# The mixture-of-experts stage of a float32 network: experts ranked on chip, run in pairs of a large and a small one, the four smallest in two matrix passes instead of three

## The chip, the cores and the metric

The kernel runs on one core of one Trainium2 chip. The metric is the device time of one execution in microseconds (us). Before the change it is 1656.29 us, the median of three runs (1655.75 to 1657.96). Engines are named as in the profile: PE is the matrix engine (PEld its weight loads), DVE the vector engine, ACT the scalar engine, POOL the GpSimd engine, SP the engine that issues most transfers.

## The reference, cut to what matters

Two blocks of a network are computed for 256 tokens of width 1024, in float32. All but the last stage stay as they are. The last stage is a mixture of experts: each token goes to its two best of eight experts, and the outputs are added with softmax gates; then a layer norm follows.

```python
def moe_swiglu(h, router, wg, wu, wd):
    logits = (t @ router)
    vals, idx = lax.top_k(logits, TOP_K)            # TOP_K = 2 of N_EXPERTS = 8
    gates = softmax(vals)
    combine = sum(one_hot(idx, N_EXPERTS) * gates[..., None], 1)
    for e in range(N_EXPERTS):                      # D_EXPERT = 1408
        out += combine[:, e:e + 1] * swiglu(t, wg[e], wu[e], wd[e])

def swiglu(t, wg, wu, wd):
    return (silu(t @ wg) * (t @ wu)) @ wd
h = layer_norm(ALPHA * h + out, ln2_g, ln2_b)
```

The 256 tokens choose 512 times in all. Worked out from the reference for the inputs drawn with seed 0, the eight experts get 110, 80, 89, 28, 21, 35, 109 and 40 tokens.

## The kernel before

**Weights.** All weights of the kernel come as one stream of 311 units of 1 MB, each 16 tiles of 128x128 in float32. A unit's way is: SP loads it into one of four buffers `stg` (NS = 4); ACT copies it, rounded to the PE's one-pass float format, to `wh` (one of three buffers, NW = 3, line 1223); DVE writes the remainder `wl = stg - wh` (line 1723); PE multiplies. ACT may write `wh` of unit u only when PE is done with unit u-3 (the semaphore event `("unit", u - NW)`), and SP may load unit u only when ACT and DVE are both done with unit u-4. The activations are split in the same way into a high and a low part, and each product is made of three matmuls: high x `wh`, low x `wh`, high x `wl` (lines 981 to 983 for gate and up, 1012 to 1014 for down). ACT and DVE run their splits at fixed places of their programs: the class `Splits` issues the split of unit u+2 where the walk over the tiles enters unit u.

**Experts.** They begin with unit 179 (`EXPERT_UNIT`); one takes 16.5 units: for gate and up, 11 column tiles in groups of 4, 4 and 3 (`GU`), each with 8 steps over the width, and for down 11 steps for each of two halves of 512 columns. `route()` finds each token's two experts, its place in the expert's list (`rk`) and the longest list (`CNT`). If this is at most 128, the arm `sparse()` runs, otherwise `every_token()`, in which each expert takes all 256 tokens. In `sparse()` the tokens of an expert are gathered by matmuls with a selection matrix `SE` (line 1053; from `XTH` and `XTL` to `GH` and `GL`, 128 rows an expert, whatever its count), and the results go back through `SX` (`ST` in the rows; `scatter`, lines 1065 and 1066), which DVE adds to `RES` (line 2348). The tokens are the stationary operand of the matmuls (128 columns of it), the weights stream. Between gate/up and down stand silu on ACT (line 1602), the product with up on DVE (`hidden`, line 2323), its transposition on PE (`turn`, line 962), and the split of the result on ACT (line 1586) and DVE (line 2306). `select` (lines 1037, 1039) makes `SX` and the token's gate `CO`. The eight experts run one after another, in their own order; scatter, gather and select of neighbours are put between the groups of gate/up.

**What sets the order.** Each engine's program is written out by hand, and each engine runs its own in order; there is no scheduler. A wait in front of an instruction holds back everything behind it on that engine.

Of the kernel before, what the change touches and what calls it, by code (L numbers as in the profile page):

```python
# [8 lines left out]
F32 = mybir.dt.float32  # L9
F32R = mybir.dt.float32r  # L10
# [5 lines left out]
P = 128  # L16
# [99 lines left out]
class Dry:  # L116
# [14 lines left out]
    def __le__(self, other):  # L131
        return self
# [33 lines left out]
DOWN = [(0, kt) for kt in range(8)] + [(1, kt) for kt in range(8)] + [(0, kt) for kt in range(8, 11)] + [(1, kt) for kt in range(8, 11)]  # L166
# [7 lines left out]
def low_event(j, q):  # L174
    return "gathered_low_a" if j == 0 and q >= 2 else "gathered_low"
# [13 lines left out]
def model_kernel(nc, w_d, x_d, meta_d, small_d, const_d, look_d, tab1_d, tab2_d, out_d):  # L189
# [3 lines left out]
    with ctx:  # L193
# [79 lines left out]
        with ExitStack() as st:  # L273
            C8 = sb("C8", [P, 10, 2, 8], F32, st)
            CNT = sb("CNT", [P, 9], F32, st)
            CNI = sb("CNI", [P, 1], I32, st)
            XTH = sb("XTH", [P, 2, D], F32R, st)
# [4 lines left out]
            with ExitStack() as sp:  # L282
                SX = [sb(f"ST{i}", [P, S], F32R, sp) for i in range(2)]
                GH = [sb(f"GH{i}", [P, KD, 2 * P], F32R, sp) for i in range(2)]
                GL = [sb(f"GL{i}", [P, KD, 2 * P], F32R, sp) for i in range(2)]
                SHH = [sb(f"SHH{i}", [P, 11, P], F32R, sp) for i in range(2)]
                SHL = [sb(f"SHL{i}", [P, 11, P], F32R, sp) for i in range(2)]
                CO = sb("CO", [P, 2], F32, sp)
# [112 lines left out]
        def tensor_program(w, pe):  # L401
# [506 lines left out]
            def route():  # L908
# [41 lines left out]
                keep_warm(3)  # L950

            def gate_up(tag, x, nT, lh, ll, operand, turned, between):
                pend = []

                def turn():
                    while pend:
                        gi, n0, nn, i, j = pend.pop(0)
                        b, old = bank((tag, "ht", x, gi, i), (f"h_low_{tag}", (x, gi, i)))
                        vacant(old)
                        w.wait_ge(*m.of(f"hidden_{tag}", (x, gi, i)))  # L960
                        for c in range(nn):
                            ins = pe.transpose(PS[b][:, c * P:(c + 1) * P], mtm2[j][:, c * P:(c + 1) * P], ident)
                        ins.then_inc(*m.inc(f"group_{tag}", ("ht", x, gi, i)))

                for gi, (n0, nn) in enumerate(GU):
                    for up in range(2):
# [1775 lines left out]
```

## Time and profile before

| what | before |
|---|---|
| median of three runs | 1656.29 us |
| span of the profiled execution, first to last instruction | 1654.0 us |
| experts' stage (first expert matmul to the last) | 1229.2 to 1635.3 us |
| two experts with all that stands between them | 102.6 us |
| PE busy in the stage | all of it but about 1 us |
| granted PE clock | 1.00 to the last stretch |

The profiled execution has no time of its own beside its span; the 2.3 us between span and median are taken as what lies around the span, and the sum is made against the span and carried over to the median. A matmul's duration in a row is longer than its share of PE, since matmuls overlap: what one costs is the distance between two starts. DVE and ACT rows carry some 0.08 us of tail, which the next instruction overlaps.

### The profile page before, as it was taken

The numbers are of one execution on the slowest core, as the hardware profiler recorded it, in microseconds if no ns is written. First come the engines' busy times: TensorE is split into PE (matmuls) and PEld (weight loads), VectorE is DVE, ScalarE is ACT, GpSimd is POOL, SyncE is SP. The second block draws the span as 40 slices with busy tenths as digits, with TensorE's granted clock in tenths as the row PEclk, the third lists the DMA queues.
The fourth block names the chain that finished last, engine by engine and source line by source line (L and its number), as shares of the span: only waits on it lengthen the run. The fifth ranks groups of instructions, "written<-read, shape, count | busy, mean of one in ns | idle before, by whom it ended". The sixth has DMA issues, their size and how long they took to land.

```text
span 1654.0 us, 27617 instructions
## 1 busy us (share of the span) xinstructions
PE 1622.1 (98%) x11068; PEld 1477.6 (89%) x11068; DVE 1241.3 (75%) x1766; ACT 972.3 (59%) x1381; POOL 309.1 (19%) x307
## 2 busy tenths in 40 slices
PE   8999999999999999999999999999999999999997
PEld 6988888898888889998999999999998888888886
DVE  5565776656567656898875554799988898898897
ACT  6556675446657634555554443555558677777675
POOL 1231552123217501143120002132110000000000
PEclk9999999999999999999999999999999999999999
DMA  8632455555235554543435544543428898988993
GB/s 289 234 115 103 168 189 194 181 199 183 110 133 198 179 202 176 177 150 114 168 119 190 176 179 178 170 154 128 179 100 340 328 352 340 340 333 330 351 342 126
DMA packets 50198, 339.76 MB, mean 205 GB/s; under 512 B 5576, under 2 KB 7840, under 8 KB 10352
## 3 DMA queue, kind: packets, MB, share of 16 engines
q1 hardware_dynamic: 47344, 328.79, 54.0%
q0 software_dynamic: 2720, 9.13, 1.8%
q8 instruction: 91, 1.49, 0.4%
q14 instruction: 43, 0.34, 0.1%
HBM read 336.76 MB, written 1.13 MB: 204 GB/s over the span
## 4 chain that ended last, share of the span: by engine, by line
PE 90%; DVE 4%; ACT 3%; POOL 1%; issue 1%; DMA 0%; SPq 0%; DVEq 0%; POOLq 0%; ACTq 0%
PE bank L549 12%; PE bank L523 8%; PE bank L525 8%; PE bank L524 8%; PE bank L547 7%; PE bank L981 5%; PE bank L982 5%; PE bank L983 5%; PE bank L680 3%; PE bank L682 3%; PE bank L681 3%; PE bank L1014 2%; PE bank L1013 2%; PE bank L1012 2%; DVE wl L1723 1%
## 5 line engine op out<-in xcount | busy, mean ns | idle before, releaser
L1723 DVE TENSOR_TENSOR wl<-stg,wh 128x2048 fp32r<-128x2048 f32 x310 | 712.7, 2302 | 212.0 <-ACT wh L1223 209.8
L1223 ACT ACTIVATE wh<-stg 128x2048 fp32r<-128x2048 f32 x310 | 592.6, 1912 | 180.2 <-PE bank L983 82.5
L523 PE MATMUL bank<-xx,wh 128*128 128x272 f32 (+1 forms) x778 | 225.6, 290 | 0.0
L525 PE MATMUL bank<-xx,wl 128*128 128x272 f32 (+1 forms) x778 | 223.3, 287 | 0.0
L524 PE MATMUL bank<-xx,wh 128*128 128x272 f32 (+1 forms) x778 | 223.1, 287 | 0.0
L549 PE MATMUL bank<-xx,wh 128*128 128x512 f32 x448 | 159.7, 396 | 0.0
L549 PE MATMUL bank<-H,wh 128*128 128x512 f32 x434 | 151.3, 390 | 0.0
L524 PEld LDWEIGHTS bank<-xx,wh 128*128 128x128 f32 x778 | 147.5, 190 | 0.0
L981 PE MATMUL bank<-wh,GH 128*128 128x512 f32 (+3 forms) x400 | 147.5, 369 | 0.0
L523 PEld LDWEIGHTS bank<-xx,wh 128*128 128x128 f32 x778 | 146.3, 188 | 1.1 <-issue 0.7
L982 PE MATMUL bank<-wh,GL 128*128 128x512 f32 (+3 forms) x400 | 146.5, 366 | 0.0
L525 PEld LDWEIGHTS bank<-xx,wl 128*128 128x128 f32 x778 | 146.3, 188 | 0.0
L983 PE MATMUL bank<-wl,GH 128*128 128x512 f32 (+3 forms) x400 | 146.1, 365 | 0.0
L680 PE MATMUL bank<-wh,xx 128*128 128x256 f32 x480 | 139.7, 291 | 1.4 <-DVE zm L1797 0.8
L682 PE MATMUL bank<-wl,xx 128*128 128x256 f32 x480 | 134.7, 281 | 0.0
L681 PE MATMUL bank<-wh,xx 128*128 128x256 f32 x480 | 134.5, 280 | 0.0
L547 PE MATMUL bank<-xx,wl 128*128 128x256 f32 x512 | 132.4, 279 | 0.1
L547 PE MATMUL bank<-H,wl 128*128 128x256 f32 x448 | 124.0, 282 | 0.0
L2525 POOL TENSOR_TENSOR fu<-ft 128x256 f32<-128x256 f32 x64 | 84.9, 1330 | 134.2 <-ACT ft L1371 134.2
L2083 DVE SCALAR_TENSOR_TENSOR CA<-HC,small,CA 128x272 f32<-128x272 f32 x240 | 107.4, 500 | 0.7
L547 PEld LDWEIGHTS bank<-xx,wl 128*128 128x128 f32 x512 | 96.5, 188 | 5.9 <-issue 0.3
L680 PEld LDWEIGHTS bank<-wh,xx 128*128 128x128 f32 x480 | 90.2, 188 | 12.0 <-issue 9.0
(386 smaller groups left out, 3550.7 us busy)
## 6 DMA issues: line engine op xcount, KB each, us to landing
stg<-in_w SPq DMA_DIRECT2D x310, 1024.0 KB, 4.8
BT<-bias_scratch POOLq DMA_DIRECT2D x3, 1024.0 KB, 11.4
BT<-bias_scratch POOLq DMA_DIRECT2D x1, 2048.0 KB, 12.8
BB<-bias_scratch POOLq DMA_DIRECT2D x2, 1024.0 KB, 6.3
res<-in_x SPq DMA_DIRECT2D x1, 1024.0 KB, 6.4
stg<-in_w SPq DMA_DIRECT2D x2, 512.0 KB, 7.9
BB<-bias_scratch POOLq DMA_DIRECT2D x2, 512.0 KB, 7.0
out<-res SPq DMA_DIRECT2D x4, 256.0 KB, 3.1
```

What stands on the lines that cost most here:

```text
L523: pe.matmul(out, wh, xh(kt), start=kt == 0, stop=False)
L524: pe.matmul(out, wh, xl(kt), start=False, stop=False)
L525: ins = pe.matmul(out, wl, xh(kt), start=False, stop=kt == KT - 1)
L547: ins = pe.matmul(PS[b][:, 0:S], wl, high(kt), start=False, stop=False)
L549: ins = pe.matmul(out, wh, both(kt), start=False, stop=kt == KT - 1)
L680: pe.matmul(out, xh_t(kt, tt), wh, start=kt == 0, stop=False)
L682: ins = pe.matmul(out, xh_t(kt, tt), wl, start=False, stop=kt == KD - 1)
L981: pe.matmul(out, lh(kt, i), wh, start=kt == 0, stop=False)
L982: pe.matmul(out, ll(kt, i), wh, start=False, stop=False)
L983: ins = pe.matmul(out, lh(kt, i), wl, start=False, stop=kt == KD - 1)
L1223: act.activation(WH[u % NW][:, :], stg[u % NS][:, :], ACT.Copy).then_inc(*m.inc("w_high", u))
L1723: vec.tensor_tensor(WL[u % NW][:, :], stg[u % NS][:, :], WH[u % NW][:, :].bitcast(F32), ALU.subtract).then_inc(*m.inc("w_low_v", u))
```

## The change

1. **Ranking.** After the router, DVE orders the experts by their counts: expert 0 is put first always (its first weights are loaded before the counts are known), the others follow by count (`TIE`, `CNT`, `POS`, `PERM`). The arm `sparse()` is taken if each of the first four has at most 128 tokens and each of the last four at most 64 (`TWICE`, `NEED`).
2. **Pairs.** The experts run as four pairs (rank 0 with 4, 1 with 5, 2 with 6, 3 with 7). Within a pair the groups alternate: gate and up of a column group for the large one, then for the small one; in down they change after every 4 steps, which is one unit.
3. **Two passes.** A small expert's 64 tokens stand twice in the stationary operand, 64 columns of high and 64 of low parts, so that high x `wh`, low x `wh`, high x `wl` and low x `wl` take two matmuls (`in_two`). The two halves of the result are added by a plain float32 matmul with a stacked identity (`BOTH`, `turn_and_sum`), which also transposes; for it ACT copies both results from the bank to `ROWS`. Silu and product come after that, on 64 columns a tile.
4. **Addresses.** The experts' weights lie in two tensors of their own (`units`, 16 units an expert, and `tails`, the half unit that is left); SP loads seven expert numbers into registers (`WHICH`) and issues each load with a computed address.
5. **Around.** The gather of the first large expert (`lead`) stands in `route()` ahead of the branch, that of the first small one in the stage; a gather has 192 columns instead of 256, and all of its copies are on ACT. The scatters of a pair are summed in the bank, so that DVE adds half as often. `last_norm` sums the variance over four tiles instead of two folded ones, and the last scatter stands in the middle of its mean.

```diff
-DOWN = [(0, kt) for kt in range(8)] + [(1, kt) for kt in range(8)] + [(0, kt) for kt in range(8, 11)] + [(1, kt) for kt in range(8, 11)]
+DOWN = [(g, kt) for g in range(2) for kt in range(11)]
+FEW = 64
...
+            def in_two(both, last):
+
+                def product(out, kt, wh, wl):
+                    pe.matmul(out, both(kt), wh, start=kt == 0, stop=False)
+                    return pe.matmul(out, both(kt), wl, start=False, stop=kt == last)
+                return product
...
+                def turn_and_sum(x, gi):
+
+                    b, old = bank(("sp", "ht", x, gi, 0), ("hidden_sp", (x, gi, 0)))
+                    vacant(old)
+                    w.wait_ge(*m.of("both"))
+                    for up in range(2):
+                        w.wait_ge(*m.of("up_rows" if up else "gate_rows", (x, gi, 0)))
+                        for c in range(GU[gi][1]):
+                            o = up * 256 + c * FEW
+                            ins = pe.matmul(PS[b][:, o:o + FEW], ROWS[up][:, c * P:(c + 1) * P], BOTH[:, :], start=True, stop=True)
...
+                    for gi in range(3):
+                        def small_turned(kt):
+                            if kt == 2 and gi > 0:
+                                turn_and_sum(few_, gi - 1)
+
+                        rows("sp", big, gi, 0, [large], "gate_sp", large_ready if gi == 0 else nothing, small_turned)
+                        if gi == 0 and j == 0:
+                            gather_small()
+                        if gi == 0 and j > 0:
+                            scatter(j - 1, (2, 3))
+                        if gi > 0 and j < PAIRS - 1:
+                            gather(j + 1, 2 * gi - 2)
+                        rows("sp", big, gi, 1, [large], "hidden_sp", nothing, nothing)
+                        if gi > 0 and j < PAIRS - 1:
+                            gather(j + 1, 2 * gi - 1)
+                        rows("sp", few_, gi, 0, [small_], "gate_rows", small_ready if gi == 0 else nothing, nothing)
+                        turn("sp", big, gi, 0, 0)
+                        if gi == 1:
+                            select(big)
+                            select(few_)
...
+                        rows("sp", few_, gi, 1, [small_], "up_rows", nothing, nothing)
...
+                def rows_out(x, gi, up):
+                    n = GU[gi][1] * P
+                    w.wait_ge(*m.of("group_sp", ("gu", x, gi, up, 0)))
...
+                if (j, i) == (0, 4):
+                    w.wait_ge(*m.of("which"))
+                    chosen = [0] + [w.eng.value_load(WHICH[0:1, rank_of(x):rank_of(x) + 1], min_val=1, max_val=7) for x in range(1, 8)]
+                if PAIR_UNITS[i] is not None:
+                    s, n = PAIR_UNITS[i]
+                    sync.dma_start(stg[u % NS][:, :], expert_rows(units_d, chosen[2 * j + s] * 16 + n)).then_inc(*m.dma(f"w_in{u % NS}", u))
```

**Where instructions move, first place: the first expert(s), after the up part of the second column group.** On PE there stood, before, the transposition of the hidden values behind the gate part of the next group (8 steps of three matmuls) and right after it the next gather (`xc` holds the hidden values, `consts` the identity):

```order
L981 MATMUL bank<-wh,GH 128x384
L982 MATMUL bank<-wh,GL 128x384
L983 MATMUL bank<-wl,GH 128x384
L962 MATMUL bank<-consts,xc 128x128 [waits s_hidden_sp,s_slots_out]
L962 MATMUL bank<-consts,xc 128x128 x3
L1053 MATMUL bank<-SE,XTH 128x256 [waits s_gate_sp]
L1053 MATMUL bank<-SE,XTH 128x256 x3
L1053 MATMUL bank<-SE,XTL 128x256 [waits s_h_low_sp]
L1053 MATMUL bank<-SE,XTL 128x256 x3
L981 MATMUL bank<-wh,GH 128x384 [waits s_slots_out]
```

After the change it stands behind the gate part of the small expert, whose steps are pairs of matmuls (lines 989 and 990, `G` holds the gathered tokens):

```order
L989 MATMUL bank<-wh,G 128x512
L990 MATMUL bank<-wl,G 128x512
L1025 MATMUL bank<-consts,xc 128x128 [waits s_hidden_sp,s_gate_sp]
L1025 MATMUL bank<-consts,xc 128x128 x3
L1069 MATMUL bank<-consts,SE 128x128 [waits s_combine_sp]
L1069 MATMUL bank<-consts,SE 128x128
L1071 MATMUL bank<-SHARE,SE 128x1 x2
L1069 MATMUL bank<-consts,SE 64x128 [waits s_gathered_high]
L1069 MATMUL bank<-consts,SE 64x128
L1071 MATMUL bank<-SHARE,SE 64x1 x2
```

Between the end of up and the transposition PE had 24 matmuls and has 16 now, of the same width. On DVE, at the first column group, the order before is this (line 1723 is the split, 2323 the hidden product, 2306 the split of the transposed values):

```order
L1723 TENSOR_TENSOR wl<-stg,wh 128x2048 [waits s_w_high] x2
L2323 TENSOR_TENSOR xc<-xc,bank 128x512 [waits s_gate_sp,s_group_sp]
L2230 TENSOR_SCALAR SE<-consts,C 128x128 x2
L1723 TENSOR_TENSOR wl<-stg,wh 128x2048 [waits s_w_high] x2
L2306 TENSOR_TENSOR SHL<-bank,SHH 128x512 [waits s_h_high_sp]
L1723 TENSOR_TENSOR wl<-stg,wh 128x2048 [waits s_w_high] x2
```

and after the change (line 1895 is the split, 2522 and 2530 the same two for the large expert, 2562 and 2568 those of the small one):

```order
L1895 TENSOR_TENSOR wl<-stg,wh 128x2048 [waits s_w_high] x2
L2522 TENSOR_TENSOR xc<-xc,bank 128x512 [waits s_gate_sp,s_group_sp]
L1895 TENSOR_TENSOR wl<-stg,wh 128x2048 [waits s_w_high] x2
L2530 TENSOR_TENSOR SHL<-bank,SHH 128x512 [waits s_h_high_sp]
L1895 TENSOR_TENSOR wl<-stg,wh 128x2048 [waits s_w_high] x3
L2562 TENSOR_TENSOR xc<-xc,bank 128x256 [waits s_gate_sp]
L1895 TENSOR_TENSOR wl<-stg,wh 128x2048 [waits s_w_high]
L2568 TENSOR_TENSOR SHB<-xc,SHB 128x4x64 [waits s_h_high_sp]
```

The hidden product stands behind the same two splits in both; the small expert's come later, one split apart.

**Second place: the end of `route()`, where the arm is chosen.** On PE the count is loaded right behind the warm-keeping matmuls (line 431), before:

```order
L431 MATMUL bank<-consts 128x256 [waits s_logits]
L431 MATMUL bank<-consts 128x256 x2
L1155 TENSOR_LOAD CNI [waits s_count_in]
L1157 COMPARE_AND_BRANCH
L1053 MATMUL bank<-SE,XTH 128x256 [waits s_chosen,s_xt_high]
L1053 MATMUL bank<-SE,XTH 128x256 x3
```

and after:

```order
L444 MATMUL bank<-consts 128x256 x2
L973 MATMUL bank<-SE,XTH 128x128 [waits s_chosen,s_xt_high]
L973 MATMUL bank<-SE,XTH 128x128 x7
L973 MATMUL bank<-SE,XTH 128x128 [waits s_xt_high,s_rank]
L973 MATMUL bank<-SE,XTH 128x128 x7
L973 MATMUL bank<-SE,XTL 128x128 [waits s_xt_low]
L973 MATMUL bank<-SE,XTL 128x128 x7
L973 MATMUL bank<-SE,XTL 128x128 [waits s_xt_low]
L973 MATMUL bank<-SE,XTL 128x128 x7
L1260 TENSOR_LOAD CNI [waits s_count_in]
L1262 COMPARE_AND_BRANCH
L981 MATMUL bank<-wh,G 128x512 [waits s_w_high,s_w_low_v,s_lead_low,s_lead_high]
```

The last eight gather matmuls ahead of the load wait for DVE's last two `XTL` tiles. These stand on DVE right behind the count, before:

```order
L2230 TENSOR_SCALAR SE<-consts,C 128x128
L2275 TENSOR_REDUCE CNT<-bank 128x1 [waits s_group]
L2277 CAST CNI<-CNT 128x1 [waits s_count]
L2230 TENSOR_SCALAR SE<-consts,C 128x128 x2
L2236 TENSOR_TENSOR XTL<-bank,XTH 128x512 [waits s_xt_high] x4
L2446 TENSOR_LOAD CNI [waits s_count_in]
```

and after the change behind the ranking:

```order
L2465 TENSOR_SCALAR TWICE<-POS 128x8 [waits s_v_step]
L2466 TENSOR_TENSOR PERM<-POS,consts 128x64
L2469 TENSOR_TENSOR NEED<-TWICE,bank 128x8 [waits s_v_step]
L2471 TENSOR_REDUCE NEEDED<-NEED 128x1 [waits s_count]
L2473 CAST CNI<-NEEDED 128x1 [waits s_v_step]
L2475 TENSOR_TENSOR xc<-PERM,consts 128x64 [waits s_order]
L2477 TENSOR_REDUCE NUMBER<-xc 128x8 [waits s_v_step]
L2479 CAST WHICH<-NUMBER 128x8 [waits s_v_step]
L2412 TENSOR_TENSOR XTL<-bank,XTH 128x512 [waits s_xt_high] x2
L2704 TENSOR_LOAD CNI [waits s_count_in]
```

Eleven small operations of the ranking lie on DVE between the first two `XTL` tiles and the last two.

## Rows read from the trace of the kernel before

**Rows 1.** The page: its first line.
```profile
span 1654.0 us, 27617 instructions
```

**Rows 2.** Windows: stretch, busy time by engine, clock, DMA share, GB/s.
```profile
100.00:105.00 5.00, 3.86 (x29) 2.72 (x28) 2.12 (x1) 3.60 (x7) 1.82 (x2) 1.00 0.39 161
1246.20:1348.80 102.60, 102.60 (x532) 89.31 (x531) 92.22 (x65) 75.78 (x61) 0.00 (x0) 1.00 0.88 338
```

**Rows 3.** Groups by shape, 1230 to 1654 us: count, busy, mean ns.
```profile
L1723 DVE TENSOR_TENSOR wl<-stg,wh 128x2048 fp32r<-128x2048 f32 x131 | 299.5, 2291 | 39.7 <-ACT wh L1223 37.4
L1223 ACT ACTIVATE wh<-stg 128x2048 fp32r<-128x2048 f32 x129 | 247.5, 1919 | 103.5 <-PE bank L983 82.5 <-PE bank L1014 20.7
L981 PE MATMUL bank<-wh,GH 128*128 128x512 f32 x255 | 100.5, 394 | 0.0
L1012 PE MATMUL bank<-wh,SHH 128*128 128x512 f32 x176 | 69.2, 393 | 0.0
L981 PE MATMUL bank<-wh,GH 128*128 128x384 f32 x112 | 38.2, 341 | 0.0
L2348 DVE TENSOR_TENSOR res<-res,bank 128x512 f32<-128x512 f32 x32 | 20.4, 681 | 0.0
L2386 DVE SCALAR_TENSOR_TENSOR xx<-bank,CO,xx 128x512 fp32r<-128x512 f32 x16 | 11.7, 746 | 3.1 <-ACT xx L1662 3.1
```

**Rows 4.** Timeline of PE: start, us, line, operation.
```profile
1293.09 0.39 PE L983 MATMUL bank<-wl,GH 128*128 128x512 f32 x1
...
1295.81 0.39 PE L983 MATMUL bank<-wl,GH 128*128 128x512 f32 x1
...
1311.04 0.34 PE L983 MATMUL bank<-wl,GH 128*128 128x384 f32 x1
...
1312.60 0.33 PE L983 MATMUL bank<-wl,GH 128*128 128x384 f32 x1
```

**Rows 5.** Chain that ended last: start, us on it, line and count.
```profile
1220.57 1.79 PE bank L918 x16
1240.33 0.34 PE bank L1039 x4
1246.25 0.44 PE bank L962 x4
1252.85 0.95 PE bank L1053 x8
```

**Rows 6.** Timeline of ACT and DVE behind the first expert's first up.
```profile
1240.21 1.92 ACT L1223 ACTIVATE wh<-stg 128x2048 fp32r<-128x2048 f32 x1 [0.80 <-PE bank L983]
1242.16 2.29 DVE L1723 TENSOR_TENSOR wl<-stg,wh 128x2048 fp32r<-128x2048 f32 x1 [0.43 <-ACT wh L1223]
1244.37 0.68 DVE L2323 TENSOR_TENSOR xc<-xc,bank 128x512 f32<-128x512 f32 x1
1244.97 0.60 DVE L2230 TENSOR_SCALAR SE<-consts,C 128x128 fp32r<-128x128 f32 x2
```

**Rows 7.** Transfers and SP's waits, 1230 to 1654 us; one window of 3 us.
```profile
stg<-in_w SPq DMA_DIRECT2D x127, 1024.0 KB, 4.9
SPq L143 <- DVE wl L1723: 366.5, 127, 28.2
1240.00:1243.00 3.00, 3.00 (x18) 2.58 (x17) 2.57 (x2) 2.77 (x2) 0.00 (x0) 1.00 1.00 418
```

**Rows 8.** Timeline of DVE and PE at the end of the routing.
```profile
1222.62 0.17 DVE L2267 TENSOR_TENSOR C<-C 128x16 f32<-128x16 f32 x1
1222.83 0.17 DVE L2269 TENSOR_REDUCE C<-C 128x2 f32<-128x16 f32 x1
1224.12 0.15 DVE L2277 CAST CNI<-CNT 128x1 int32<-128x1 f32 x1
1224.70 2.48 DVE L2236 TENSOR_TENSOR XTL<-bank,XTH 128x512 fp32r<-128x512 f32 x4
1225.13 2.15 PE L1053 MATMUL bank<-SE,XTH 128*128 128x256 f32 x16
```

More of the change, by code:

```diff
@@ L1008, in down, with rows @@
+            def rows(tag, x, gi, up, products, read, operand, each):
+                nn = GU[gi][1]
+                bs = [bank((tag, "gu", x, gi, up, i), (read, (x, gi, i))) for i in range(len(products))]
+                for kt in range(KD):
+                    operand(kt)
+                    pieces = pieces_of(at[0], nn)
+                    for i, product in enumerate(products):
+                        b, old = bs[i]
                         if kt == 0:
                             vacant(old)
-                        if g == 0:
-                            w.wait_ge(*m.of(f"h_low_{tag}", (x, min(kt // 4, 2), i)))
@@ L1047, in gather @@
                         vacant(old)
-                        w.wait_ge(*m.of("xt_low" if hl else "xt_high", (1, q // 2)))
+                        w.wait_ge(*m.of("chosen", 1))
+                        for kt in range(KD):
+                            for tt in range(2):
+                                ins = pe.matmul(PS[b][:, kt * FEW:(kt + 1) * FEW], (XTH, XTL)[hl][:, tt, kt * P:(kt + 1) * P], SE[0][:, tt, 0:FEW],
+                                                start=tt == 0, stop=tt == 1)
@@ L1100, in every_token @@
+                last_norm("sp", "added", [(3, f) for f in range(4)], lambda: scatter(3, (2, 3)))
             def every_token():
@@ new lines, in route @@
+                w.wait_ge(*m.of("consts_in"))
+                act.activation(BOTH[0:FEW, :], ident[0:FEW, 0:FEW], ACT.Copy).then_inc(*m.inc("both", 1))
+                act.activation(BOTH[FEW:P, :], ident[FEW:P, FEW:P], ACT.Copy).then_inc(*m.inc("both", 0))
+                for hl in range(2):
+                    for h in range(2):
+                        w.wait_ge(*m.of("group", ("lead", hl, h)))
+                        act.activation(G[0][:, 4 * h:4 * h + 4, 2 * P * hl:2 * P * hl + P], bank(("lead", hl, h))[:, :].rearrange("p (a b) -> p a b", a=4),
+                                       ACT.Copy).then_inc(*m.inc("lead_low" if hl else "lead_high", h))
@@ new lines, in route, with in_order @@
+                w.wait_ge(*m.last("v_step"))
+                vec.tensor_copy(WHICH[:, :], NUMBER[:, :]).then_inc(*m.inc("which", 0))
+                for tt in range(2):
+                    turned_low(tt, 1)
+            def in_order(out, table, step):
+                four, every = [P, 2, 8, 8], R8[:, 0, :, :, :]
+                vec.tensor_tensor(every, table.unsqueeze(2).to_broadcast(four), PERM[:, :, :].unsqueeze(1).to_broadcast(four),
+                                  ALU.mult).then_inc(*m.step(step))
+                w.wait_ge(*m.last(step))
+                return vec.tensor_reduce(out, every, AX, ALU.add)
```

838 lines of the change are left out of this document (503 added, 335 removed).

## The prediction

> **What bounds the kernel now.** I read the windows of the experts' stage first, then its groups by shape, the chain, and single stretches of the timeline. The reader is to see in the window of two experts [rows 2] that PE is busy for all of 102.60 us, with DVE at 92.2, ACT at 75.8 and DMA at 0.88. So PE sets the pace and work taken from PE shortens the stage; but DVE and the transfers stand so close behind that they decide how much. The long DVE group waited 37 us in all for ACT, and ACT 103 us for PE [rows 3]: both waits follow PE's pace and aren't its cause. SP waited for DVE to free a buffer [rows 7], which is a wait for the pace too.
>
> **The price list.** Between the two starts at 1293.09 and 1295.81 lie twelve matmuls of 512 columns, 2.72 us [rows 4]: 0.227 each, so a unit of three-pass work is 12 x 0.227 = 2.72 and one of two passes 8 x 0.227 = 1.82. Nine of 384 columns lie between 1311.04 and 1312.60: 0.173 each [rows 4]. On the chain [rows 5] a transposition costs 0.44/4 = 0.11; eight gather matmuls of 256 columns 0.95, or 0.119 each; two float32 matmuls with one column (four records) 0.34, or 0.17 each; eight float32 matmuls of 128 columns (16 records) 1.79, or 0.22 each. A split costs DVE 2.21, from its start to the next instruction's (1242.16 to 1244.37), and ACT some 1.85 without its tail [rows 3, 6].
>
> **PE in a pair.** One pass of one expert is 32 + 22 matmuls of 512 columns (255 in gate/up and 176 in down, over eight experts [rows 3]) and 16 steps of 384: 54 x 0.227 + 16 x 0.173 = 15.0 us. The small expert loses one pass: -15.0. Its 11 transpositions (1.2) become 22 float32 matmuls of 64 columns. The trace has none of these; the bounds are 0.17 (one column) and 0.22 (128 columns), so 3.7 to 4.8; I take 0.19, between them, 4.2: +3.0. Select before was 4 transpositions and 4 one-column matmuls (1.1); now 6 float32 matmuls of 128 columns and 6 of one, 2.3: +1.2. The gather's 32 matmuls shrink from 256 to 192 columns; by the columns 0.09 each, at worst 0.119 as before: -0.9 (0 to -0.9). The scatter has as many matmuls as before. Sum: 102.6 - 15.0 + 3.0 + 1.2 - 0.9 = 90.9 us of PE work in a pair, 11.7 less.
>
> **Where PE will wait.** DVE in a pair: 33 splits x 2.21 = 72.9; four adds of scatters at 0.60 net, half of before, 2.4; four outputs at 0.67, 2.7; hidden and split of the large expert, six operations of 384 or 512 columns, 3.3; the same for the small one, six of 256 or 192 columns, between 0.2 and 0.6 each, 1.9; four selections 1.2. Sum 84.4 of 90.9, so DVE doesn't bind on the mean. It binds in order. Take t = 0 where PE ends a large expert's up part. Only then is a buffer free for the split of the third small unit: ACT until 1.9, DVE until 4.1, and the hidden product stands behind that split, until 4.7. The trace shows just this: ACT's split starts at 1240.21 when PE frees the buffer, the hidden product ends at 1244.97, 4.8 later [rows 6]. Before, PE had 2 x 2.72 = 5.4 us of gate work in this gap, and didn't wait. Now it has 2 x 1.82 = 3.6, plus 0.7 of gather where there is one: it waits 1.1 us in the first group and 0.3 in the second; in the third, where half of three units is 1.5 x 1.82 = 2.7 (+0.7), it waits 1.2. Next, DVE's two splits behind the hidden product end at 6.9 and 9.1, where PE, having done the small gate, turn and up, would want the next large unit at 8.8: 0.3 more in the first group, none in the second, which has the selects' 2.3 in it. Then `turn_and_sum` after three steps of the next gate wants `ROWS`, and ACT copies the up half only behind its next 1.9 us split: late by about 0.3, 0.8 and, in down, where it stands after one step, 1.9. In down a large and a small unit take PE 4.54 and DVE 4.42 plus its outputs and adds: over 11 units DVE has 28.7 us, PE 25.0 of passes, 1.2 and 1.9 of sums and scatter, 28.1: 0.6 more; and the next pair's first group has 21.3 on DVE (eight splits, four selections, two adds, hidden and split) against 20.5 on PE: 0.5. Sum of waits: 1.1 + 0.3 + 1.2 + 0.3 + 0.3 + 0.8 + 1.9 + 0.6 + 0.5 = 7.0 us a pair. Each is a difference of two longer times and off by perhaps a third, and a wait at one point lets DVE catch up for the next; I keep 1.5 to 10 as ends. A pair is then 97.9, 4.7 less; four are 18.8 less. The last pair has moves of 2.7 us on DVE but no gather, as before.
>
> **The head.** Before, the small chained operations on DVE stand 0.21 apart [rows 8], and the count was there at 1224.3. Now two `XTL` tiles (1.2 of the 2.48 [rows 8]), then eleven small operations (2.5) and two more tiles (1.2) end at about 1229.1. PE's last eight gather matmuls of `lead` wait for them. The load of the count and the branch took at most 0.8 (1224.3 to 1225.13 [rows 8]) and stand behind these matmuls. The first expert matmul starts at about 1230.0, not 1229.2: +0.8. The small expert's gather, 32 matmuls of 64 columns, isn't in the trace; from nothing to 0.119 each, I take 0.07, near the columns' share plus the load: +2.3. SP must wait for `WHICH` (1228), load seven registers at up to 0.8 each, and only then loads unit 183, which it had before at once: it lands by 1239, in time, but 184 to 186 follow late, and DVE's selections for the next pair come just then: PE waits for the second small unit, +1.5 (0 to 4). The head is +4.6.
>
> **The tail.** A scatter of 16 matmuls stands now between the halves of the mean, and the mean's first half fills the wait for the last expert's output; two more float32 matmuls replace one fold on DVE. I take 0, with 1 either way.
>
> **Sum.** 1654.0 - 18.8 + 4.6 = 1639.8 for the span [rows 1]; with the 2.3 us between span and median, 1642. I give 1641, since the waits partly pay for each other.
>
> **The transfers.** A pair loads 33 units of 1.049 MB. At 338 GB/s and a share of 0.88 [rows 2] the full rate is some 384 GB/s, 90 us a pair; a window of 3 us shows 418 at a share of 1.00 [rows 7], 83 us. I take the second as nearer to the limit, since it is a rate that was reached; a pair of 97.9 then has 5 to 15 us to spare. The Trainium skill (DMA: Bandwidth & Descriptors, on the iDMA fabric, in its table of load streams) gives 408.7 GB/s for one stream of 1 MiB loads issued from SP; by it, as an estimate, a pair can't be under 84.7 us. The trace agrees, with 418 over 3 us.
>
> **The rivals.**
> - *The buffers swallow the waits* (chance 0.2). Two units of `wh` and four of `stg` lie ahead; if the waits above fall together to 1.5 a pair, a pair is 92.4: 1656.3 - 40.8 + 4.6 = 1620. For it: before, DVE ran at 90% and PE didn't wait at all. Against it: the 4.8 us of rows 6 are a chain that no buffer shortens.
> - *The weights' way becomes the bound* (0.19). ACT has ten more copies a pair (rows to `ROWS`, gathers), each ahead of some split; if PE waits 10 us a pair, a pair is 100.9: 1656.3 - 6.8 + 4.6 = 1654. Mostly still faster, in part within what can be told.
> - *Late loads, slower than before* (0.07). Each load now needs address arithmetic on SP between wait and issue. The ring of a `stg` buffer is 4.9 (landing [rows 7]) + 1.9 + 2.2 + some 0.3 of hand-over = 9.3 us for four units, 2.33 a unit. It decides if a unit takes over (102.6 - 1.1)/33 = 3.08, that is if a load is late by 4 x 3.08 - 9.3 = 3.0 us. If it were 4: 3.33 a unit, 110 a pair, 1656.3 + 29.6 + 4.6 = 1690. No row has an instruction of SP that costs anything like it.
> - *The clock* (0.02). PE would have waits of up to 2 us in every group. If the clock went to 1.2 GHz in the three small phases of a pair (7 us each), +20 a pair: about 1720. Against it: between 100 and 105 us PE was busy for 3.86 of 5.00 us and the granted clock was 1.00, the level of 2.4 GHz [rows 2]. The Trainium skill (TensorE: Matmul & The Clock Gate, HAM oscillation) warns that waits for data between short stretches of matmuls let the clock fall each time; by it these waits could cost far more than their length. No row here shows a wait like those with a lowered clock.
> - *The other arm* (0.02). If a count doesn't fit, every expert takes 256 tokens in three passes, 90 us instead of 51: some 310 us more, 1960. The reference's counts (40, 35, 28, 21 in the small places, 110 the largest) fit.
>
> **How the numbers follow.** My forecast has 0.5, with 1632 to 1650 as its own range (waits of 5 to 9 a pair). What a measurement of this kernel can tell is about 0.2%, 3.3 us: under 1653.0 is faster. All of the first two cases and 0.12 of the third lie there: 0.82. Within: 0.08, from the third. Slower: the rest, 0.10. The range leaves out half of the second case and the slow rivals: 1620 to 1657.
>
> **What the profile after would show.** Steps right: PE's busy time in a pair near 91 us of some 98; pairs of equal length; the transposition (line 1025) waiting about 1 us for the hidden product; `turn_and_sum` waiting for ACT's `ROWS`; float32 matmuls of 64 columns near 0.19; the first expert matmul near 1230.0 and the landing still near 5 us. It would be wrong if ACT shows waits for loads (then the transfers bind), if the clock row falls under 1.00 inside the stage, if PE has no waits (then 1620), or if the 64-column matmuls cost 0.3 and more, which adds 2.4 us a pair.

## The result and the profile after

| | median us | runs from to | ratio to before (95%) |
|---|---|---|---|
| before | 1656.47 | 1655.67 to 1658.06 | |
| after | 1662.38 | 1660.30 to 1670.69 | 1.0044 (1.0031 to 1.0058) |

The forecast was 1641 and faster; the changed kernel is 0.44% slower by the ratio of the runs, 5.9 us by the medians, and 21 us over the forecast. Its profiled execution is one of its slow ones, 1670.3 us, 8 over its median; the page's first line gives the span, where before had 1654.0 [rows 1].

```profile
span 1668.5 us, 27751 instructions
```

The windows of three pairs, from one first `turn_and_sum` to the next, answer to [rows 2] (columns as there):

```profile
1261.40:1365.40 104.00, 96.79 (x504) 81.96 (x503) 84.72 (x58) 76.49 (x71) 0.00 (x0) 0.98 0.91 329
1365.40:1468.20 102.80, 95.77 (x504) 80.39 (x503) 86.37 (x58) 75.77 (x67) 0.00 (x0) 1.00 0.93 338
1468.20:1573.10 104.90, 97.26 (x504) 81.56 (x503) 84.91 (x54) 77.52 (x68) 0.00 (x0) 0.98 0.92 335
```

A pair was to shrink from 102.6 to 97.9 and lasts 102.8 to 104.9. PE is no longer busy all the time, so the lighter work is there; it bought waits. The DMA share, 0.88 before, is 0.91 to 0.93 at no more GB/s than before's 338, and two pairs have a mean clock of 0.98. (In the trace of experiment 1, the same kernel but for its addresses and at a clock of 1.00 in all three pairs, they last 100.5, 102.3 and 101.7 us, so of the 104 some 2 are the clock's.)

The groups by shape, 1230 to 1650 us, beside [rows 3] (us in total, mean ns, idle ahead and its causes):

```profile
L1895 DVE TENSOR_TENSOR wl<-stg,wh 128x2048 fp32r<-128x2048 f32 x131 | 297.8, 2289 | 74.5 <-ACT wh L1326 73.3
L1326 ACT ACTIVATE wh<-stg 128x2048 fp32r<-128x2048 f32 x129 | 246.7, 1917 | 98.7 <-PE bank L983 53.5 <-DMA stg<-in_units 33.3 <-PE bank L990 7.3
L1109 PE MATMUL bank<-BOTH,ROWS 128*128 128x64 f32 x176 | 23.8, 280 | 6.1 <-ACT ROWS L1727 5.7
```

ACT's splits waited only for PE before; now they wait 33.3 us for loads (`stg<-in_units`). The list of waits, 1262 to 1630 us (us in total, times, longest), names the other two:

```profile
ACT wh L1326 <- DMA stg<-in_units: 30.9, 31, 2.3
...
PE bank L1025 <- DVE xc L2522: 14.3, 11, 2.4
...
PEld bank L1109 <- ACT ROWS L1727: 7.5, 10, 1.7
```

L1025 is the transposition in `turn`, waiting for the hidden product; L1109 is `turn_and_sum`, waiting for `ROWS`. The transfers of the same stretch (KB each, median us from issue to landing), 4.9 before [rows 7]:

```profile
stg<-in_units SPq DMA_DIRECT2D x114, 1024.0 KB, 6.8
```

At the head, PE's timeline has the last wait of the routing and the small expert's gather, and four windows have the clock:

```profile
1229.62 1.11 PE L973 MATMUL bank<-SE,XTL 128*128 128x128 f32 x8 [0.79 <-DVE XTL L2412]
...
1237.94 1.87 PE L1082 MATMUL bank<-SE,XTH 128*128 128x64 f32 x16
1239.64 2.17 PE L1082 MATMUL bank<-SE,XTL 128*128 128x64 f32 x16
```

```profile
1231.00:1234.00 3.00, 3.00 (x8) 2.30 (x7) 2.90 (x7) 0.36 (x1) 0.00 (x0) 0.50 0.18 27
1234.00:1237.00 3.00, 3.00 (x13) 2.40 (x12) 2.63 (x9) 1.60 (x1) 0.00 (x0) 0.93 0.86 344
...
1240.00:1243.00 3.00, 3.00 (x18) 2.76 (x18) 2.86 (x5) 1.19 (x3) 0.00 (x0) 0.70 0.99 382
1243.00:1246.00 3.00, 3.00 (x11) 2.39 (x10) 0.22 (x2) 0.00 (x0) 0.00 (x0) 0.73 1.03 355
```

A clock of 0.50 is the level of 1.2 GHz: the first row has only 8 matmuls of 512 columns in its 3 us, where at 0.23 each there is room for 13. The gather of 32 narrow matmuls lasts from 1237.94 to the next matmul's start at 1241.62, 3.7 us or 0.115 each.

### The profile page after: what moved, and what is told of

The parts are those of the page before. It is cut to its first block, busy times and chain, and to the rows that moved or that the text cites. A ratio compares the mean times of both kernels' runs of the same rounds, so it can differ in the third digit from the quotient of the medians.

```text
span 1668.5 us, 27751 instructions
## 1 busy us (share of the span) xinstructions
PE 1608.2 (96%) x10996; PEld 1454.8 (87%) x10996; DVE 1218.1 (73%) x1751; ACT 981.1 (59%) x1419; POOL 309.0 (19%) x307
## 4 chain that ended last, share of the span: by engine, by line
PE 76%; ACT 8%; DVE 7%; DMA 4%; issue 3%; POOL 1%; SPq 0%; DVEq 0%; ACTq 0%; POOLq 0%
PE bank L562 12%; PE bank L536 8%; PE bank L538 8%; PE bank L537 8%; PE bank L560 7%; ACT wh L1326 5%; DVE wl L1895 4%; DMA stg<-in_units 4%; PE bank L693 3%; PE bank L694 3%; PE bank L695 3%; PE bank L981 2%; PE bank L983 2%; PE bank L982 2%; PE bank L444 1%
## 5 line engine op out<-in xcount | busy, mean ns | idle before, releaser
L537 PEld LDWEIGHTS bank<-xx,wh 128*128 128x128 f32 x778 | 147.5, 190 | 0.0
L536 PEld LDWEIGHTS bank<-xx,wh 128*128 128x128 f32 x778 | 146.3, 188 | 1.1 <-issue 0.7
L693 PEld LDWEIGHTS bank<-wh,xx 128*128 128x128 f32 x480 | 90.5, 188 | 10.9 <-issue 8.7
L562 PEld LDWEIGHTS bank<-xx,wh 128*128 128x128 f32 x448 | 84.1, 188 | 17.2
L562 PEld LDWEIGHTS bank<-H,wh 128*128 128x128 f32 x434 | 81.5, 188 | 16.8
L694 PEld LDWEIGHTS bank<-wh,xx 128*128 128x128 f32 x480 | 90.5, 189 | 0.1
## 6 DMA issues: line engine op xcount, KB each, us to landing
BT<-bias_scratch POOLq DMA_DIRECT2D x3, 1024.0 KB, 10.4
```

The costliest lines, as they stand in the source:

```text
L536: pe.matmul(out, wh, xh(kt), start=kt == 0, stop=False)
L537: pe.matmul(out, wh, xl(kt), start=False, stop=False)
L562: ins = pe.matmul(out, wh, both(kt), start=False, stop=kt == KT - 1)
L693: pe.matmul(out, xh_t(kt, tt), wh, start=kt == 0, stop=False)
L694: pe.matmul(out, xl_t(kt, tt), wh, start=False, stop=False)
```

## The experiments

Times are medians in us; a ratio is to runs of before taken beside the experiment (their medians are 1655.8 to 1656.6). After I saw the result, my theory was that three things cost the 21 us together: the loads, the waits ahead of the turn, and PE work that I had priced too low.

**1. Fixed addresses.** SP's seven register loads go; the order found on chip is written into the program.

```diff
-                    w.wait_ge(*m.of("which"))
-                    chosen = [0] + [w.eng.value_load(WHICH[0:1, rank_of(x):rank_of(x) + 1], min_val=1, max_val=7) for x in range(1, 8)]
+                    chosen = [(0, 6, 2, 1, 7, 5, 3, 4)[rank_of(x)] for x in range(8)]
```

> The changed kernel with the experts' numbers as constants in SP's program (the same order, the same loads): no register loads, no address arithmetic, no wait for the ranking on SP. Theory A (the way of the weights bounds: loads that overlap land later, 6.8 us instead of 4.9, because they come in bunches, not because of their addresses): 0 to 4 us less than the changed kernel's 1662, all of it at the head, landing unchanged near 6.8. Rival L (address arithmetic makes each load late): 12 us less or more, landing back to 4.9. Rival B (the order of the instructions makes PE wait): as theory A.

1662.59, ratio 1.0036 (1.0024 to 1.0049): nothing. Loads by loaded addresses cost nothing that can be told here, and the landing is 6.6 us.

**2. Half the loads.**

```diff
-                    sync.dma_start(stg[u % NS][:, :], expert_rows(units_d, chosen[2 * j + s] * 16 + n)).then_inc(*m.dma(f"w_in{u % NS}", u))
+                    sync.dma_start(stg[u % NS][:, 0:HALF], expert_rows(units_d, chosen[2 * j + s] * 16 + n)[:, 0:HALF]).then_inc(*m.dma(f"w_in{u % NS}", u))
...
-                    sync.dma_start(stg[u % NS][:, 0:HALF], expert_rows(tails_d, chosen[2 * j])).then_inc(*m.dma(f"w_in{u % NS}", ("tail", u)))
```

The unit that two experts share loses its first half in the same way.

> The changed kernel with only the first half of each expert unit loaded (the buffers' other half keeps old values, so the output isn't the reference's); ACT, DVE and PE work unchanged. Theory A: a pair of experts falls from 104 to 98 us or less, 1640 or under. Rival B: the waits of PE for hidden values and rows stay, 1655 to 1662. Rival C (the clock falls while PE waits): as B, and the granted clock stays under 1.00 in the same places.

1656.77, ratio 1.0011 (0.9997 to 1.0026), runs from 1654.0 to 1663.3: in rival B's range. The second half of the loads is worth 5.6 us, and even without it the change gains nothing. Its trace is the cleanest view of PE's own sequence, since its pairs are alike (100.24, 101.61 with a stretch of lowered clock, 100.26; the first runs from the first `turn_and_sum` at 1257.61 to the one at 1357.86). Two places of PE's timeline:

```profile
1257.61 1.89 PE L1109 MATMUL bank<-BOTH,ROWS 128*128 128x64 f32 x16
1259.32 0.47 PE L981 MATMUL bank<-wh,G 128*128 128x512 f32 x1
...
1349.00 0.40 PE L990 MATMUL bank<-wl,G 128*128 128x512 f32 x1
1351.29 0.63 PE L1025 MATMUL bank<-consts,xc 128*128 128x128 f32 x4 [1.89 <-DVE xc L2522]
```

Eight matmuls of 64 columns (16 records) take 1.71 us from start to start, 0.214 each. The turn of a pair's first group starts 2.29 us after the last matmul ahead of it, where 0.23 is usual. Add up the distances between PE's starts in that pair, by shape, and set apart what exceeds the median of its shape by over 0.3: of 100.2 us 5.5 are such gaps (ahead of the three turns 0.63, 1.31 and 2.06; in `down` 0.53 and 0.92). Of the remaining 94.8, `ROWS` waits inside the sums are 0.9. That leaves 93.9 of work. The same sum over the pair of before in [rows 2] gives 102.6 and no gap.

**3. The third pass given back** to the small expert (its weights' low half multiplied twice, so the product is altered).

```diff
                     pe.matmul(out, both(kt), wh, start=kt == 0, stop=False)
+                    pe.matmul(out, both(kt), wl, start=False, stop=False)
                     return pe.matmul(out, both(kt), wl, start=False, stop=kt == last)
```

> The changed kernel with a third matmul in each step of the small experts (high x low weights twice, so the output isn't the reference's): 15 us more PE work a pair, nothing else. If PE's own work set the pace, +60 us. Theory A and rival B both have 12 us of waits a pair that it would fill: a pair becomes about 106 us, +8 to +20 in all; under rival B the waits for hidden values go to zero, since PE again has 5.4 us in the gap; under A some waits for weights stay. Rival C: the clock no longer falls but at the head, so the time may even be unchanged.

1693.67, ratio 1.0219 (1.0200 to 1.0239): 60 us more work cost 31, over the 8 to 20 expected; a pair lasts 109.9 and not 106, and has 0.6 us of gaps left. The rest of the work went into what had been waits. PE's wait for the hidden product fell to 0.6 us in the stage, ACT's for loads to nothing, and the landing to before's (transfers, and one window of the stage):

```profile
stg<-in_units SPq DMA_DIRECT2D x99, 1024.0 KB, 5.0
```

```profile
1262.00:1362.00 100.00, 99.44 (x533) 86.32 (x532) 76.85 (x52) 71.34 (x67) 0.00 (x0) 1.00 0.86 313
```

So slow landing and waits both come with the two-pass rhythm; the new instructions, which all stand here too, don't bring them by themselves.

**4. The lighter work alone, in the old order.** The kernel before, with one product skipped in every second expert, in `down` as shown and in the same way in gate and up.

```diff
-                        pe.matmul(PS[b][:, :], hl(kt, i), wh, start=False, stop=False)
+                        if tag == "et" or x % 2 == 0:
+                            pe.matmul(PS[b][:, :], hl(kt, i), wh, start=False, stop=False)
```

> The kernel before, with the matmul low tokens x high weights left out for the four odd experts (the output isn't the reference's): 15 us less PE work for each two experts, the old order, fixed addresses. Theory A: loads can't be faster than some 370 GB/s once they overlap, a pair not under 94 to 97: 1622 to 1634. Rival B (the new order is what waits): the old order waits only where DVE's 2.6 us a unit is longer than PE's 1.82, a pair of 51 + 42 = 93 to 94 us, 1620; if neither holds and ACT or DVE chains bind as in the new order, over 1640.

1639.81, ratio 0.9906 (0.9873 to 0.9939), runs from 1634.4 to 1646.0: above theory A's range, and at the edge of rival B's last case. Of 60 us removed 16.5 came back as time. Here too ACT waits for loads, and they land late (waits and transfers, 1262 to 1600 us):

```profile
ACT wh L1225 <- DMA stg<-in_w: 46.0, 55, 2.7
```

```profile
stg<-in_w SPq DMA_DIRECT2D x115, 1024.0 KB, 6.6
```

**5. Two matmuls ahead of the wait at the head**, `keep_warm(2)` before the fourth quarter of `lead`.

> In the changed kernel PE stands idle for 0.79 us at 1229.62, where the last eight matmuls of the large expert's first gather wait for XTL, and from 1231 the granted clock is 0.50 to 0.93, again at 1240 to 1246 (0.70, 0.73). Here two matmuls of 256 columns on constants stand in front of that wait and fill it; nothing else changes. Theory (the idle moment at the head brings the lower clock on, some 3 us of it): no stretch under 1.00 between 1230 and 1246, and 2 to 3 us less, 1659.5. Rival (the clock falls for another reason, such as the many narrow matmuls of the small expert's gather): the clock rows stay and the time stays at 1662.4, or grows by the 0.1 to 0.3 us by which the two matmuls overrun the wait.

1664.53, ratio 1.0056 (1.0039 to 1.0073). The clock did what the theory said and the time what the rival said: in the profiled execution all windows from 1231 to 1246 stand at 1.00, yet nothing was gained. One of them, beside the 0.70 above:

```profile
1240.00:1243.00 3.00, 3.00 (x15) 2.43 (x14) 1.80 (x5) 0.97 (x1) 0.00 (x0) 1.00 1.02 431
```

That the two matmuls kept the clock up isn't shown by it. In the traces of experiments 2, 6 to 10 and 12 the same wait of 0.79 stands there and the clock stays at 1.00 behind it; in those of 1 and 3 it falls. So that wait alone isn't what brings the lower level on. What does stays open.

**6, 7. The turn four steps later,** with whole and with half loads. On ACT `high(big, gi)` and on DVE `low(big, gi)` move with it.

```diff
-                        turn("sp", big, gi, 0, 0)
...
-                        rows("sp", few_, gi, 1, [small_], "up_rows", nothing, nothing)
+                        def turn_here(kt):
+                            if kt == 3:
+                                turn("sp", big, gi, 0, 0)
+                        rows("sp", few_, gi, 1, [small_], "up_rows", nothing, turn_here)
```

> The turn of the large expert's hidden part is moved four steps back, into the small expert's up rows, with its copy on ACT and its subtraction on DVE; nothing is added or taken away. With half the loads, PE still waited ahead of this turn 0.63, 1.31 and 2.06 us in a pair (starts of its last matmul to the next, less the usual distance), 4.0 us. Theory A (the wait for the hidden product is a third of the loss, and its place is the cause): those three waits go, a pair shrinks by 2.5 to 4 us, and the time is 1662.4 - 12 = 1650 (1646 to 1653). Rival B (the weights' way is full: DMA share 0.92 to 0.95 and splits that wait for stg): PE waits for wh or wl instead, the pair shrinks by under 1 us, 1658 to 1662. Rival C (DVE and ACT are only reordered, and the split of the hidden part comes too late for down): new waits at the first steps of down, 1660 or more.

1659.80, ratio 1.0021 (1.0008 to 1.0034), runs from 1654.0 to 1663.5: in rival B's range.

> The kernel with the later turn, and of each expert's weight unit only the first half is loaded (the other half of the buffer keeps old weights, so this part of the product is computed from wrong weights). With the turn at its old place half the loads gave 1656.8. Theory A (PE's order costs 4 us a pair whatever the loads do): 1656.8 - 14 = 1643 (1640 to 1646), so 5 to 9 us under the same kernel with whole loads. Rival B (the loads are what binds once the turn is moved): the gap between this kernel and the one with whole loads grows from 5.7 to 12 us or more. Rival C (the wait only moves into down): about 1655 here too.

1645.88, ratio 0.9942 (0.9925 to 0.9958), runs from 1645.2 to 1646.9, and the gap of 13.9 that rival B named. The later turn is worth 2.6 us with whole loads and 10.9 with half: each limit hid the other. The wide spread belongs to the whole loads too.

**8. Half of the sums left out.**

```diff
                     for up in range(2):
                         w.wait_ge(*m.of("up_rows" if up else "gate_rows", (x, gi, 0)))
+                    for up in range(1):
                         for c in range(GU[gi][1]):
```

> Leaves out the eleven float32 matmuls of 64 columns a pair that sum the small expert's up rows (the gate's sum is used in their place); the copies to ROWS and all waits stay. In the trace 22 such matmuls take 5.65 us of a pair (eight take 2.06), 0.257 each where the forecast had 0.19. Theory (they stand on PE's path one for one): 11 x 0.257 x 4 = 11.3 us less, 1651. Rival (PE waits elsewhere by as much as it saves, as when the third pass was added and 60 us more work cost 31): half of it, 1657. Second rival (they cost nothing net, since PE waits for the splits anyway): 1662.

1663.60, ratio 1.0043 (1.0030 to 1.0057): nothing. But this edit does more than leave work out. In the changed kernel the gate's sums run first and fill the time until the up rows are there; here they too stand behind the wait for `up_rows`. In a pair at full clock, `turn_and_sum` with the wait ahead of it is 0.3 us shorter (6.3 in experiment 2, 6.0 here), though 11 x 0.214 = 2.4 us of matmuls are gone. So the run doesn't tell what these matmuls cost. The 0.257 in the expectation was 5.65/22 and had 0.9 us of `ROWS` waits in it; the matmul itself is 0.214.

**9, 10. A fifth `stg` buffer,** alone and with the later turn (its room comes from laying `ACC` over `SQ`, which is idle in the stage). Theory by now: not the rate of the transfers, but the four buffers in a ring.

```diff
+FIFTH = EXPERT_UNIT + 4
+def buffer_of(u):
+    return u % NS if u < FIFTH else (4, 3, 0, 1, 2)[(u - FIFTH) % 5]
```

> A fifth stg buffer for the experts' weight units, from the fifth unit of the stage on; order and work stay. Known by now: with half the loads the changed kernel took 1656.8, with the later turn 1659.8, with both 1645.9, so one limit hides behind the other; the DMA share in the stage is 0.92 to 0.95 at 335 to 345 GB/s, while single stretches reach 0.98 and 363 to 370. Theory R (the ring of four buffers leaves the queues empty for 5 to 8% of the time, as a buffer comes free only when DVE has split it): the DMA share rises to 0.97 or more, the wait of wh for stg (30.9 us) falls below 15, and the time falls towards that of half loads, 1657 to 1659 here, where the waits ahead of the turn stay. Rival D (about 340 GB/s is what two overlapping loads get on the chip in this stage): the landing grows with the fifth load in flight, share and GB/s stay, and so does the time, 1662.

1656.97, ratio 1.0009 (1.0000 to 1.0019).

> The fifth stg buffer and the later turn together. The later turn alone gave 1659.8, with half the loads 1645.9. Theory R (the ring of four buffers starves the queues): up to 13.9 us are to be had, I expect 1650 (1647 to 1655), under both kernels. Rival D (the rate of the transfers is the bound whatever the number of buffers): 34.6 MB a pair at 343 GB/s are 101 us, so 1658 to 1661.

1647.34, ratio 0.9946 (0.9930 to 0.9963), runs from 1644.1 to 1648.0: 15.0 under the changed kernel and 0.54% under before, with the whole computation. The two factors side by side:

| us | turn at its place | turn later |
|---|---|---|
| four buffers | 1662.4 | 1659.8 |
| half the loads | 1656.8 | 1645.9 |
| five buffers | 1657.0 | 1647.3 |

A fifth buffer does what half the loads do, to 1.5 us, and in the pairs exactly: 100.25 us in experiments 2 and 9, 98.6 in 7 and 10. With five buffers the transfers thus no longer hold anything up. (In the profiled executions, 3 of the 10.6 us between the stages of experiments 9 and 10 are two stretches of lowered clock in 9 that 10 doesn't have; a full pair went from 100.25 to 98.6.) ACT's wait for loads, 30.9 us, is 0.4 with it and nothing with both; the share expected for the fifth buffer (0.97 or more) didn't come. First a window of experiment 9, then two of 10:

```profile
1262.00:1362.00 100.00, 94.74 (x504) 80.26 (x503) 85.07 (x57) 77.70 (x71) 0.00 (x0) 1.00 0.93 345
```

```profile
1240.00:1246.00 6.00, 6.00 (x28) 4.68 (x27) 3.47 (x6) 3.61 (x2) 0.00 (x0) 1.00 1.01 426
...
1262.00:1362.00 100.00, 96.51 (x514) 81.89 (x514) 86.42 (x58) 78.57 (x72) 0.00 (x0) 1.00 0.95 354
```

The transfers make 345 to 354 GB/s over a pair and 426 over 6 us. In experiment 10 part of the wait ahead of the turn has moved to the small expert's weights (PE's timeline):

```profile
1346.52 0.40 PE L997 MATMUL bank<-wl,G 128*128 128x512 f32 x1
1348.21 0.47 PE L996 MATMUL bank<-wh,G 128*128 128x512 f32 x1 [1.29 <-DVE wl L1906]
```

**11. Control: the fifth buffer in the kernel before** (laid over `SQ`, which is idle in the stage).

> Control: the kernel before, with a fifth stg buffer for the experts' units. In its expert stage PE is busy 20.00 of 20.00 us in nearly every stretch. Theory R (the fifth buffer helps only where PE waits for splits or for what stands behind them): within 0.2% of 1656.0. Rival (the buffer speeds the stage up by itself): 1650 or less, and then the 1647.3 of the fifth buffer with the later turn would say little about the change.

1657.71, ratio 1.0005 (0.9996 to 1.0015): nothing, as PE doesn't wait there.

**12. Experiments 8 and 10 together.**

> The kernel with the fifth buffer and the later turn (1647.3), and the eleven matmuls of 64 columns a pair that sum the small expert's up rows left out (the gate's sum is used in their place). With four buffers and the turn at its place, leaving them out changed nothing (1663.6 against 1662.4). Theory R (PE's own sequence is the bound once the ring has five buffers): 11 x 0.257 x 4 = 11.3 us, less what ACT and DVE then hold up: 8 to 11 less, 1638. Rival (the splits or the transfers are the next bound at once; 34.6 MB a pair at 353 GB/s and share 0.95): under 4 us less, 1644 or more.

1644.82, ratio 0.9931 (0.9915 to 0.9948): 2.5 less, the rival's time. PE's work in a pair fell by 2.4 us, yet the pair went from 98.6 to 98.3, and waits for `ROWS` stand in its place (list of waits, 1262 to 1630 us):

```profile
PEld bank L1117 <- issue: 12.2, 11, 1.5
PE bank L1117 <- ACT ROWS L1738: 8.2, 11, 1.2
```

They are the edit's own, as in experiment 8. PE's timeline at the same place of the second pair, first experiment 10, then 12 (the second of the three rows in each is `turn_and_sum`):

```profile
1379.52 0.34 PE L990 MATMUL bank<-wl,G 128*128 128x384 f32 x1
1379.70 2.23 PE L1116 MATMUL bank<-BOTH,ROWS 128*128 128x64 f32 x16
1381.74 0.42 PE L988 MATMUL bank<-wh,G 128*128 128x384 f32 x1
```

```profile
1379.58 0.34 PE L990 MATMUL bank<-wl,G 128*128 128x384 f32 x1
1380.98 1.08 PE L1117 MATMUL bank<-BOTH,ROWS 128*128 128x64 f32 x8 [1.06 <-ACT ROWS L1738]
1381.86 0.42 PE L988 MATMUL bank<-wh,G 128*128 128x384 f32 x1
```

From row to row that is 2.22 and 2.28 us: what was left out came back as a wait. Over the three sums of a pair it is 5.96 and 5.64, and these 0.3 us are all that the pair lost. So neither this experiment nor 8 tells whether PE's own sequence is the bound.

**13. Experiment 4 with the fifth buffer.**

> The kernel before, with the product of the low inputs and high weights left out in four of its eight experts (so their result is less exact), which gave 1639.8 (1634.4 to 1646.0), and the fifth stg buffer. There 60 us less of PE work brought 16.5. Theory R (the ring of four buffers swallowed a part of it): some 10 us less, 1630, and a narrower spread. Rival (DVE's order of splits and hidden products holds PE up whatever the loads do): 1637 to 1640.

1629.39, ratio 0.9842 (0.9826 to 0.9858), runs from 1629.1 to 1631.9: 10.4 less and a narrow spread. The ring had swallowed that in the old order as well. Without the ring the light work brings 27 of its 60 us, and DVE is then near full (window of the stage):

```profile
1362.00:1462.00 100.00, 95.06 (x481) 79.00 (x481) 95.69 (x69) 76.73 (x60) 0.00 (x0) 1.00 0.95 364
```

## Why the prediction was wrong

Two steps failed. One is **the transfers**, which the sum had at nothing: "a pair of 97.9 then has 5 to 15 us to spare", because 418 GB/s is reached. (By its own figures, 90 and 83 us, it is 8 to 15.) That rate holds for some us; over 100 us no kernel here passed 365, or 95 us a pair. And a rate was the wrong measure. A load starts only when DVE has split what was in its buffer, so what counts is the ring. In a pair of 97.9 one buffer comes round every 4 x 97.9/33 = 11.9 us. With before's landing it takes 9.3, as the prediction itself worked out for another rival; with the landing of 6.8 it takes 11.2. That is 0.7 us of room on the mean, and an uneven stretch makes ACT wait. With five buffers the room is 5 x 98.6/33 - (6.5 + 4.4) = 4.0, and the wait is gone. I took the landing as fixed at 4.9, and it isn't: small units are used up every 1.8 us and come free in bursts, and their loads then overlap. By the times of issue and landing in the traces, in before 115 of the 125 loads issued between 1230 and 1615 us had one other load under way at their issue and landed after 5.1 us on the mean; after the change 84 of 125 had two or three others and took 7.1. Experiment 3, which slows the small units to before's pace, has 5.0 again; experiment 4, with none of the new code, has 6.6. Cost: 5.4 us (experiment 9); with the turn out of its way 12.5 by the fifth buffer and 13.9 by half loads. The rival "the weights' way becomes the bound" came nearest with 1654, but named ACT's copies for it; none of the runs moved those alone.

The other, larger by the sum, is **PE's work in a pair**: 93.9 and not 90.9, so 8.7 us was saved and not 11.7. Over four pairs that is 12 us. The third pass was to save 15.0 and saved 13.0: before's six passes take 91.6 us of a pair and the five that are left 78.6, since a matmul of 512 columns is at a mean distance of 0.236 in place of 0.229; why, no run shows. The small expert's sums cost 3.8 more than the transpositions that they replace, not 3.0 (a 64-column matmul is 0.214 and not 0.19), the gather saves 0.5 and not 0.9, and select costs 1.0 more and not 1.2.

**The waits**, 7.0 a pair, were right in sum (5.5 + 0.9 = 6.4 with the loads out of the way), and in place for the turn, though there 4.0 against 2.6 forecast. Of these the one ahead of the first group's turn, 2.06, was twice what I gave it, and the `ROWS` waits (0.9 against 3.0) less. With the fifth buffer the pair is thus 100.25 and not 97.9: 3.0 more of work and 0.6 less of waits, 4 x 2.35 = 9.4 us of the miss. That the turn's waits come from its place is shown by experiments 7 and 10. They take out these 4.0 us, but 2.4 come up elsewhere, and a full pair gains 1.6.

**The head**, +4.6, came out about right in sum and wrong in its parts. The start was 0 to 2.2 late, by execution, for 0.8. The small gather took 3.5 to 3.8 for 2.3, at 0.11 to 0.12 a matmul: near the 0.119 of [rows 5] with four times the columns, so such a matmul is priced by its count here, not by its columns. Late units behind the address loads, +1.5, didn't happen (experiment 1).

**The clock**, a rival at 0.02, was no rival but a surcharge: in the profiled execution it was lowered in five places of the stage, where before has none. At the two shown above, each over 6 us, PE lost some 1.7 us (3 x (0.50 + 0.07) and 3 x (0.30 + 0.27)); if the others cost as much, five are 8.5 us. The runs of the changed kernel follow it (1660.3 at a mean clock of 0.999, 1670.7 at 0.992); the runs at 0.996 lie 2 to 3 us above the one at 0.999.

The sum: 9.4 for pairs, 5.4 for the ring, 2 to 3 for the clock and about 1 for the head make 18 to 19 of the 21; the other 2 to 3 I can't assign. The 9.4 is bookkeeping from one trace, and no run took out the surplus work to see it come back. The signs that the prediction listed for its own failure, ACT waiting for loads and a clock row under 1.00, are the first two that the profile shows.

What stays open, besides the clock and the 0.236: whether less PE work would shorten a pair, which experiments 8 and 12 were to tell and don't. A pair of experiment 10 has 94.0 us of work and 4.6 of waits, the largest 1.5 for the small expert's `wl` behind the turn and 1.5 in `down`. DVE's split of 2.29 us against 1.84 for PE's eight matmuls on a small unit, with only three `wh` and `wl` buffers to even it out, may be their cause; no run moved it.

## What to carry over

Price a load ring by its round trip (landing, splits, hand-over, times units over buffers) at the new pace, with a landing measured under bursts, and not by the rate; here 0.7 us of room on the mean was too little, and 4.0 was enough. When work on the busiest engine gets lighter, list every loop that was hidden under it: here there were two of nearly one length, and removing one alone gave 5.4 and 2.6 us, both together 15.0. To find that out, remove them in pairs. And when an experiment leaves work out, keep every wait in its place: in experiments 8 and 12 a wait moved ahead of work that used to hide it, and ate the gain.

## What the runs showed of the hardware

- The landing of a 1 MiB load depends on how loads overlap: a median of 4.9 us in before at 338 GB/s, 6.8 after at up to the same rate, 5.0 with the third pass back. In the changed kernel a load issued with one other under way took 5.8 us on the mean, with two 7.0.
- The loads reach 426 GB/s over 6 us with five buffers, and with four 418 over 6 us (1236 to 1242 in the changed kernel). The Trainium skill (DMA: Bandwidth & Descriptors, iDMA fabric) gives 408.7 for such a stream alone. So over a few us the trace lies above that figure, as the 418 did that the prediction called agreement; over 100 us no kernel passed 365.
- The granted clock fell to 0.50, the level of 1.2 GHz, in single stretches of a PE that was 93% busy: at the head behind a wait of 0.79 us in some traces and not in others, and behind the head 12 times in the traces of the changed kernel and of experiments 1, 2, 5, 6, 8 and 9, each time within 1.7 us of the end of a wait of 1.5 to 2.8 us. Not every such wait had a fall behind it (in experiment 2 two of four), and the stage of experiments 3, 7, 10 and 12 has none behind the head. The Trainium skill (TensorE: Matmul & The Clock Gate, HAM oscillation) warns of falls behind waits between short stretches of matmuls, and the prediction had set that aside. The traces agree that falls come behind waits, but not with each one; what they cost was 0 to 10 us of a run.
- Seven `value_load`s and register addresses on SP cost nothing that a run could tell (1662.38 with them, 1662.59 without).
